# Stored rows scaled before they are stored, added in part by the vector engine and in part by accumulating transfers, and expert weights loaded in the order in which their buffers come free

## The reference

```python
g_top, g_idx = lax.top_k(softmax(t @ w_router_g + b_router_g), 1)        # one of 4 groups
e_top, e_idx = lax.top_k(e_logits of that group, 2)                      # two of its 8 experts
e_w = softmax(e_top) * g_top                                             # weight of each expert
for each expert e:
    hid = silu(t @ w1[e]) * (t @ w3[e]) * combine[:, e]                  # F = 256
    out = out + hid @ w2[e]
x = x + g2 * out
```

## Time and profile before

| | |
|---|---|
| time, median of 3 runs (lowest to highest) | 665.71 us (665.36 to 668.84) |
| the profiled execution's own time | 666.92 us |
| its span in the profile | 665.1 us |
| PE, DVE, ACT, POOL busy | 91%, 46%, 25%, 14% of the span |
| HBM read, written | 165.36 MB, 15.74 MB |
| weights loaded through SP's queue | 1 MB each, 23 to 24 us from issue to landing (median) |

### The profile page before, as it was taken

One profiled execution on the slowest core, in us unless ns is written; L12 is line 12 of the kernel. 1 busy time (PEld: TensorE's weight loads), 2 busy tenths in 40 slices (PEclk: granted clock), 3 DMA queues, 4 the chain that ended last, 5 costly groups with the idle time before them and its releaser, 6 DMA issues.

```text
span 665.1 us, 7868 instructions
## 1 busy us (share of the span) xinstructions
PE 604.8 (91%) x3008; PEld 361.3 (54%) x3008; DVE 304.1 (46%) x606; ACT 168.9 (25%) x368; POOL 93.7 (14%) x136
## 2 busy tenths in 40 slices
PE   2699797889999999999999989999999987989785
PEld 0444585667767677774588834454444433434233
DVE  0229989375454444119525384332232322245167
ACT  3024031034444425343202301232222211112010
POOL 2022241037600000000000020211111111100000
PEclk9999899879999999999999999999999998999899
DMA  8994945923180303051456674799999999999963
GB/s 313 398 356 176 337 146 181 378 99 126 61 320 1 127 1 127 1 191 61 183 242 272 214 312 150 299 410 422 419 421 419 420 419 419 423 418 422 387 260 127
DMA packets 41498, 173.85 MB, mean 261 GB/s; under 512 B 6268, under 2 KB 6332, under 8 KB 28660
## 3 DMA queue, kind: packets, MB, share of 16 engines
q1 hardware_dynamic: 34128, 159.40, 60.6%
q0 software_dynamic: 5744, 12.84, 5.4%
q10 hardware_dynamic: 1588, 1.10, 0.5%
HBM read 165.36 MB, written 15.74 MB: 272 GB/s over the span
## 4 chain that ended last, share of the span: by engine, by line
PE 62%; DMA 14%; DVE 8%; SPq 6%; issue 6%; POOL 3%; ACTq 1%; ACT 1%; DVEq 0%; POOLq 0%
PE bank L917 11%; PE bank L642 6%; PE bank L644 6%; PE bank L643 6%; PE bank L949 5%; DMA late<-in_w_dram 4%; DMA arena<-in_w_dram 4%; PE bank L732 4%; SPq L520 3%; POOL ss L1877 3%; DMA qkg<-in_k_norm_dram 2%; PE bank L822 2%; DMA late<-in_w_in_dram 2%; PE bank L932 2%; PE bank L823 2%
## 5 line engine op out<-in xcount | busy, mean ns | idle before, releaser
L917 PE MATMUL bank<-arena,hT 128*64 128x512 f32 x352 | 86.2, 631 | 8.5 <-DMA arena<-in_w_dram 7.5
L642 PE MATMUL bank<-hT_high,w_in_parts 128*128 128x512 f32 x160 | 67.0, 419 | 3.3 <-DVE w_in_parts L1330 3.3
L644 PE MATMUL bank<-hT_high,w_in_parts 128*128 128x512 f32 x160 | 63.7, 398 | 0.0
L643 PE MATMUL bank<-hT_low,w_in_parts 128*128 128x512 f32 x160 | 63.6, 398 | 0.0
L917 PEld LDWEIGHTS bank<-arena,hT 128*64 128x64 f32 x352 | 24.5, 142 | 50.0 <-issue 40.9
L1199 ACT COPY probs<-bank 128x512 f32<-128x512 f32 x32 | 18.7, 586 | 121.3 <-PE bank L917 121.3
L1606 DVE TENSOR_SCALAR hT<-bank,ab 128x128 f32<-128x128 f32 x64 | 21.8, 403 | 50.1 <-PE bank L902 50.1
L917 PE MATMUL bank<-late,hT 128*64 128x512 f32 x160 | 39.0, 632 | 3.6 <-DMA late<-in_w_dram 3.6
L949 PE MATMUL bank<-arena,g1b 128*64 128x512 f32 x176 | 39.7, 593 | 2.2 <-DVE g1b L1621 2.2
L932 PEld LDWEIGHTS bank<-fold,probs 128*128 128x128 f32 x256 | 32.7, 197 | 16.0 <-issue 11.4
L1364 DVE TENSOR_REDUCE st<-bank 128x2 f32<-128x256 f32 (+3 forms) x16 | 13.2, 824 | 57.9 <-PE bank L668 57.8
(11 more groups left out here) (285 smaller groups left out, 1007.0 us busy)
## 6 DMA issues: line engine op xcount, KB each, us to landing
arena<-in_w_dram SPq DMA_DIRECT2D x66, 1024.0 KB, 23.0
late<-in_w_dram SPq DMA_DIRECT2D x30, 1024.0 KB, 24.2
late<-in_w_ada_dram SPq DMA_DIRECT2D x6, 2048.0 KB, 12.7
arena<-in_w_ada_dram SPq DMA_DIRECT2D x5, 2048.0 KB, 9.6
arena<-in_w_in_dram SPq DMA_DIRECT2D x4, 2048.0 KB, 16.8
late<-in_w_in_dram SPq DMA_DIRECT2D x4, 2048.0 KB, 11.2
y_scratch<-route POOLq DMA_DIRECT2D x1, 4096.0 KB, 14.9
late<-in_w_out_dram SPq DMA_DIRECT2D x2, 2048.0 KB, 7.6
```

Source lines behind the costliest of these rows:

```text
L642: mm(bank[:, b, :], wH[:, b, k, :], hH[:, k, :], start=k == 0, stop=False)
L643: mm(bank[:, b, :], wH[:, b, k, :], hL[:, k, :], start=False, stop=False)
L644: last = mm(bank[:, b, :], wL[:, b, k, :], hH[:, k, :], start=False, stop=k == 7)
L917: last = mm(bank[r, 2 + n % 2, :].rearrange("p (w f) -> p w f", w=2), xgT[n // 2 % 2][:, k, SLOTS * (n % 2):SLOTS * (n % 2 + 1)], w13[s][: ...
```

## The change

It has three parts, all in the expert stage.

1. **Scaled rows.** The combine weights of all 16 pairs are found for each slot (`combine_weights`, `weight_sums`, `weights_by_slot`), and `drain_y` multiplies with them, so that what is stored in HBM is already scaled. The weights are made ahead of the one-hot tables of group 1 instead of behind two of them, and are 128x128 wide instead of 128x16. PE has 14 more groups of four small products.
2. **Adding the rows.** SP loads only tiles 0 and 1 of the stored rows, and does so once the last w2 has landed. DVE adds them with plain additions, half of them ahead of `drain_last(1)` and half behind the last `y_low`; nothing of it stands ahead of DVE's step 31 any more. Tiles 2 and 3 are added by four accumulating transfers of 0.5 MB that POOL issues straight from HBM into `xs`: two for j = 0 once SP's loads have landed, and two for j = 1 once those have landed. The one-hot matrices `spreadT` move from `near_end` to DVE's step 29. PE gets `keep_warm` products around its last two `gate_up`.
3. **Ring loads.** `load_pair(e)` issues w1 and w3 of experts e+1 and e+2 instead of e and e+1, ahead of w2 of e and e+1.

```diff
+BY_DVE = 2
             def load_pair(e):
-                for j in range(2):
-                    sp.wait_ge(ab_done, e + j + 1 - RING)
-                    load13(e + j, (e + j) % RING)
+                for n in range(e + 1, min(e + 3, E)):
+                    sp.wait_ge(ab_done, n + 1 - RING)
+                    load13(n, n % RING)
                 sp.wait_ge(y_done, e // 2 + 1 - RING // 2)
-                for j in range(2):
-                    load2(e + j, (e + j) % RING)
+                for n in range(e, e + 2):
+                    load2(n, n % RING)
             load2(5, 5)
-            sp.wait_ge(ab_done, 2)
-            load13(RING + 1, 1)
-            sp.wait_ge(y_done, 1)
-            load2(RING, 0)
-            load2(RING + 1, 1)
-            for e in range(RING + 2, E, 2):
+            for e in range(RING, E, 2):
                 load_pair(e)
...
-            rows_of(y_d, yg_loaded)
+            sp.wait_ge(w2_loaded[(E - 1) % RING], 16 * ((E - 1) // RING + 1))
+            for t in range(BY_DVE):
+                sp.dma_start(yg[:, t], y_d[2 * P * t:2 * P * (t + 1), :].rearrange("(p j) d -> p j d", j=2)
+                             ).then_inc(yg_loaded, 16)
...
+                    if g == 1:
+                        last = weight_sums(g, q)
+            def weight_sums(g, q):
+                e = 2 * (q - IDX_GROUPS[g][0])
+                for t in range(TT):
+                    lhs = place[g][t][:, e:e + 2, :].rearrange("p e s -> p (e s)")
+                    last = mm(bank[:, 7, W0 + 6 * q:W0 + 6 * q + 6], lhs,
+                              cparts[:, t, 2 * q:2 * q + 2, :].rearrange("p e c -> p (e c)"),
+                              start=t == 0, stop=t == TT - 1)
+                return last
             keep_warm(2, 5)
             slot_sums(0)
-            keep_warm(7, 5)
+            keep_warm(5, 5)
+            pe.wait_ge(weights_ready, 1)
+            for q in IDX_GROUPS[0]:
+                weight_sums(0, q)
+            keep_warm(2, 5)
...
             one_hot(0, range(TT))
             indices(0)
+            combine_weights()
             one_hot(1, range(0, 2))
...
-                    last = v.tensor_tensor(ysb[q % 3][:, w], bank[:, 6 + h, :], g2b[:, w], ALU.mult)
+                    last = v.scalar_tensor_tensor(out=ysb[q % 3][:, w], in0=bank[:, 6 + h, :], scalar=cws[:, q:q + 1],
+                                                  in1=g2b[:, w], op0=ALU.mult, op1=ALU.mult)
...
             all_experts(step, overflow_counts, near_end)
-            for t in range(2, TT):
-                dve.wait_ge(yg_loaded[t], 16)
-                add_stored(t)
+            def add_row(t, j):
+                v.tensor_tensor(xs[:, t, :], yg[:, t, j, :], xs[:, t, :], ALU.add).then_inc(x_added, 1)
+                dve.wait_ge(x_added, BY_DVE * j + t + 1)
+            dve.wait_ge(yg_loaded, 16 * BY_DVE)
+            add_row(0, 0)
+            add_row(1, 0)
             drain_last(1)
             for h in range(2):
                 y_low(1, h)
+            add_row(0, 1)
+            add_row(1, 1)
             for n in range(2 * TT):
                 t, w = n % TT, slice(CH * (n // TT), CH * (n // TT + 1))
                 dve.wait_ge(spread_done, n + 1)
+                if t >= BY_DVE:
+                    dve.wait_ge(rows_added, 32 * (TT - BY_DVE))
                 v.tensor_tensor(xs[:, t, w], bank[:, n, :], xs[:, t, w], ALU.add).then_inc(out_ready, 1)
...
+            pool.wait_ge(yg_loaded, 16 * BY_DVE)
+            for j in range(2):
+                if j == 1:
+                    pool.wait_ge(rows_added, 16 * (TT - BY_DVE))
+                for t in range(BY_DVE, TT):
+                    pool.dma_start(xs[:, t, :], y_d[2 * P * t:2 * P * (t + 1), :].rearrange(
+                        "(p j) d -> p j d", j=2)[:, j, :], accum_op=ALU.add).then_inc(rows_added, 16)
```

More of the change, by code:

```diff
@@ L374, in hybrid_trunk @@
         y_stored = [sem(f"y_stored{i}") for i in range(3)]
-        yg_loaded = [sem(f"yg_loaded{i}") for i in range(TT)]
         y_zeroed = sem("y_zeroed")
+        weights_ready = sem("weights_ready")
+        yg_loaded = sem("yg_loaded")
+        rows_added = sem("rows_added")
         zeros_ready = sem("zeros_ready")
@@ L567, in overflow @@
                 sp.sem_inc(x_turns, 1)
[L569 to L572, removed]
             def overflow_zeros():
@@ L955, in step @@
                     fold_halves(n - 1)
+                if n >= E - 2:
+                    keep_warm(2, 0, 0, CH // 2)
                 gate_up(n)
@@ L958, in step @@
                     down(n - 2)
+                if n == E - 1:
+                    keep_warm(2, 0, 0, CH // 2)
                 if n in ROWS_AT:
@@ L1574, in indices, with combine_weights @@
                 last.then_inc(sidx_ready, 1)
[L1576 to L1580, removed]
+            def combine_weights():
+                dve.wait_ge(exp_out, 1)
+                link(v.tensor_reduce(gsum, gexp, AX.X, ALU.add))
+                link(v.reciprocal(gsum, gsum))
+                dve.wait_ge(exp_out, 2)
+                link(v.tensor_scalar(best1, edif, 1.0, None, ALU.add))
+                link(v.reciprocal(best1, best1))
+                link(v.tensor_tensor(cw[:, 0, :], best1, gsum, ALU.mult))
+                link(v.tensor_tensor(cw[:, 1, :], cw[:, 0, :], edif, ALU.mult))
+                v.tensor_tensor(cwe, oh1, bc(cw[:, 0, :], S32, 2), ALU.mult)
+                link(v.tensor_tensor(cwr, oh2, bc(cw[:, 1, :], S32, 2), ALU.mult))
                 link(v.tensor_tensor(cwe, cwe, cwr, ALU.add))
                 for c in range(3):
[L1583 removed]
+                    last = v.tensor_copy(cparts[:, :, :, c], cwe)
                     if c < 2:
+                        link(last)
                         link(v.tensor_tensor(cwe, cwe, cparts[:, :, :, c], ALU.subtract))
+                last.then_inc(weights_ready, 1)
             def weights_by_slot():
[L1588 to L1592 removed]
+                parts = bank[:, 7, W0:W0 + 6 * PAIRS].rearrange("p (q c) -> p q c", q=PAIRS)
+                for x in range(2):
+                    r = slice(SLOTS * x, SLOTS * (x + 1))
+                    v.tensor_reduce(cws[r, :], parts[r, :, 3 * x:3 * x + 3], AX.X, ALU.add)
                 v.tensor_copy(toks, tokg[:, STORED:PAIRS])
@@ L1641, in drain_last @@
                     w = slice(CH * h, CH * (h + 1))
-                    last = v.scalar_tensor_tensor(out=ysb[q % 3][:, w], in0=bank[:, 6 + h, :], scalar=cws[:, i:i + 1],
+                    last = v.scalar_tensor_tensor(out=ysb[q % 3][:, w], in0=bank[:, 6 + h, :], scalar=cws[:, q:q + 1],
                                                   in1=g2b[:, w], op0=ALU.mult, op1=ALU.mult)
@@ L1669, in near_end @@
                     y_low(0, h)
-                dve.wait_ge(tok_iota, 1)
-                for i in range(LAST):
-                    last = v.tensor_scalar(spreadT[:, i].rearrange("p t q -> p (t q)"), iota_t, toks[:, i:i + 1], None,
-                                           ALU.is_equal)
-                last.then_inc(spreadT_ready, 1)
-                dve.wait_ge(yg_loaded[0], 16)
-                add_stored(0)
-                dve.wait_ge(yg_loaded[1], 16)
-                add_stored(1)
-            def step(n):
+            def step(n):
+                if n == E - 3:
+                    dve.wait_ge(tok_iota, 1)
+                    for i in range(LAST):
+                        last = v.tensor_scalar(spreadT[:, i].rearrange("p t q -> p (t q)"), iota_t, toks[:, i:i + 1],
+                                               None, ALU.is_equal)
+                    last.then_inc(spreadT_ready, 1)
                 if n == E - 2:
```

38 lines of the change are left out of this document (10 added, 28 removed).

## The result

The changed kernel takes 674.28 us (median of 4 runs, 669.59 to 675.16); the kernel before, run beside it, 665.75 (665.36 to 668.84). The ratio, taken over all the runs and not from these two medians, is 1.0103, with a 95% interval from 1.0056 to 1.015. Three of the four runs lie between 673.9 and 675.2 and one at 669.6. The forecast was 665.0, with a range from 660.3 to 672.0: the change is slower where no change was forecast, and the time lies outside the range. The profiled execution took 673.91 us, its span was 672.1.

What follows compares the result with a forecast made beforehand. Bound by DVE's last additions, behind them the full DMA engines. Last w2 at 635.6, SP's rows 642.0, POOL's rounds until 656.7, then 7.6 and 0.1: span 664.4, forecast 665.0 us, range 660.3 to 672.0.

Steps and rivals of the forecast that it cites:

- W': Landing of the last w2 in the changed kernel: 635.6, which is 2.0 earlier than 637.6 in the kernel before.
- Stored rows by POOL: Tiles 2 and 3 at the end: two rounds of accumulating transfers, 7.2 us each, done at 656.7.
- doubled price: POOL's round if each byte costs twice because the destination is read too: 8.1 us.
- Stored rows on DVE: SP's two loads after the last w2 land at 642.0; DVE's additions and drains then run until 651.2.
- The routing sums: Small products in gate_up(1) cost PE 1.2 us, DVE's weights 1.0 more; a lower clock adds 0, bounds 0 to 1.7.
- The ring loads: Expert 8's loads go 2.2 us earlier, filling the DMA gap at 424 to 428; the stream ends 2.0 earlier.
- the ring order gives nothing: Rival: small products at the lower clock delay gate_up(2) by 3 us, last w2 stays at 637.6; 667.0 us, chance 0.09.
- PE's end: gate_up(31) starts near 631, down(30) at about 638, ending by 642 to 644; 6 to 8 us less lateness.
- The one on the slower side: Rival: POOL's accumulating transfers cost more than double; decides at a round of 9.1, 10.5 gives 671.6 us; chance 0.20.
- The plain price: Rival: POOL's accumulating transfers cost no more than plain ones, rounds of 5.6 us, 661.8 us in all; chance 0.22.

Runs made afterwards that it cites:

- e2: The changed kernel with the old order of the ring loads: 675.44 us, ratio 1.0144 to the kernel before.
- e3: The changed kernel without the sums of the combine weights for pairs 0 to 13, those rows left unscaled: 668.76 us, ratio 1.0048 to the kernel before.
- e7: The changed kernel without SP's wait for the last w2 before loading stored rows: 669.15 us, ratio 1.0046 to the kernel before.
- e4: The changed kernel with POOL's four transfers overwriting instead of adding: 666.24 us, ratio 1.0009 to the kernel before.
- e9: The changed kernel without SP's wait for the last w2, and with POOL's transfers issued once all pairs are stored: 665.39 us, ratio 1.0004 to the kernel before.
- e1: The kernel before with the new order of the ring loads alone: 661.12 us, ratio 0.994.
- e10: The kernel before with the new ring order and its eight scaled additions moved behind expert 31's hidden values; no sums, hold or POOL transfers: 660.14 us, ratio 0.9904.
- e8: The changed kernel with all four tiles loaded by SP without the hold and added by DVE, no POOL transfers: 668.17 us, ratio 1.0025 to the kernel before.
- e5: The changed kernel with POOL's transfers issued once all pairs are stored, SP's hold kept: 672.01 us, ratio 1.0085 to the kernel before.
- e6: The changed kernel with all four tiles loaded by SP, still held, and added by DVE, no POOL transfers: 671.96 us, ratio 1.0086 to the kernel before.
- e11: The kernel before with twelve more groups of four small products in gate_up(1), results unused: 668.06 us, ratio 1.002.

## Why the prediction was wrong

The chain's end reads as forecast, DVE's wait between the pieces is there, and nothing else stands on the path behind the last w2. What failed are three terms of the sum: POOL's round, put at 7.2 us, the landing of SP's rows, put at 6.4 us behind the last w2, and the cost of a lower clock behind the new sums, put at 0. Against the predicted span of 664.4 the profiled one is 7.7 longer:

| term | predicted | measured | own share |
|---|---|---|---|
| last w2 lands (W') | 635.6 | 638.38 | +2.8 |
| SP's rows land, after W' | 6.4 | 8.6 | +2.2 |
| POOL's two rounds with waits | 14.7 | 18.5 | +3.8 |
| from there to the end | 7.7 | 6.6 | −1.1 |

- **Stored rows by POOL.** "I take a value nearer the doubled one, 7.2" is the largest miss. Measured are 9.15 and 8.76, above the doubled price of 8.1; in e2, e3 and e7 the same rounds take 8.8 to 9.4. e4 splits it: plain transfers take 6.07 and 6.61, not the 5.6 made from a single transfer's fixed part, and the add costs 2.6 more per MB. Bytes twice is right in size; the fixed part of two transfers in a round was some 0.7 too small, and there was no reason to choose below the full account of bytes. That account would have given 666.8 us (the prediction says 666.9), still 7.5 too little. The Trainium skill's page "Collectives: The Full Stack", section on the bandwidth ceiling, says that the add needs two source reads, which halves the rate of a reduction. The trace agrees in size (engines busy for 5.9 against 3.1 us by the same bytes), though it does not show the second read itself, and the price of 8.1 by that rule was nearer than mine.
- **Stored rows on DVE.** "Two MB take 4.9", with 1.4 fixed, gave 6.4; 8.5 us from the first issue to the last landing were measured, and 7.3 to 7.5 in e2, e3 and e4, which hold the rows alike. The fixed part of a small transfer did not carry over to two of one MB; the other microsecond is this execution's. DVE's own part was right: its first four additions and the drain ended well ahead of POOL's rows.
- **The routing sums.** The 1.2 us of products are there (from the first L923 group of `gate_up(1)` to the transposes 9.4 us, before 8.1), and DVE's weights take 3.6 us instead of 2.75, 0.9 more where 1.0 was forecast. But "bounds: 0 to 1.7 us for the rest of the stretch [...], I take 0" for the clock failed: `gate_up(2)` alone lost 1.9, above the upper bound, and the last w2 landed 3 to 5 us later in the executions with the lower clock than in those without. This is the term behind the late W'. Besides, the router's results were 1.6 later already ahead of any changed instruction (384.20 against 382.61), which is the execution and not the change: in e4 to e9, the same code up to there, they come between 381.97 and 383.33.
- **The ring loads.** Right as a step: e1 gains 0.6% and its gap closes. The last w3, forecast at 630.7, landed at 633.5, as late as W' (two MB stand behind it, not three). In the changed kernel's profiled execution the late `gate_up(2)` ate it, which is the mechanism of the rival "the ring order gives nothing"; in e4's, with the same code there, W' was 633.8, nearly 2 earlier than forecast.
- **PE's end.** `down(30)` ended at 645.4, forecast 642 to 644; it follows W', and PE is not on the path.
- **The rivals.** The one on the slower side named the right mechanism, the price of the round twice in an uncovered chain. It was to decide at a round of 9.1. The rounds were 8.96 on average, so the sign came from them together with the two terms ahead of them: two rivals came true at once. The plain price fell with e4's comparison. What the prediction did not price by itself is the hold: it took the landing after W' as given, where e7 shows that the wait costs some 4 us.

Without the wait, and with POOL early, the change comes level (e9); with the additions left to DVE in scaled form and only moved, and the ring order kept, it becomes 1.0% faster (e10). So the good part of the change is the ring order with the order of DVE's work. The accumulating transfers and the hold gave it back, but not they alone: e8 has neither and still lies 1.2% above e10. Between these two stand the sums with the lower clock, which e3 puts at about half of that, and DVE's one wait for all four tiles (until 648.0, in e10 for the first tile until 636.4). No run takes that wait, the `keep_warm` products or the earlier `spreadT` by itself.

## What to carry to other kernels

Think twice before making work wait for the last load of a stream: here the mean DMA share was 0.33 and 0.13 while its last pieces landed, and each round behind it was paid in full. Moving additions from an engine into the transfers costs their bytes a second time plus a fixed part a round, so compare that with the engine's time, and in a DMA-bound stretch expect it back in the loads (e5: the last w2 5.6 us slower). A closed gap in one window proves nothing until the mean over the whole stretch has been looked at. When an engine's work and the loads both bound the end, try the two edits together before judging each: here one alone was worth 0.6%, the other nothing, and both 1.0%, the last step barely clear of noise. And where one profile of a version lies far from another of the same code, look at the granted clock and at several executions before giving the difference to the edit.

## What the runs showed of the hardware

- An accumulating transfer from HBM into SBUF took 2.6 us more per MB than a plain one of the same shape (rounds of 9.15 and 8.76 against 6.07 and 6.61), with the same 288 packets and 1.05 MB in the profile and the engines busy for 5.9 against 3.1 us in the first round.
- The end of a stream tails off: with one w2 load and the rest behind it under way and nothing new issued, the DMA share fell from 0.89 (624 to 628) to 0.68, 0.33 and 0.13 (636 to 638) before the last landing.
- Around and behind the groups of small products PE's granted clock was at its lower level for ten microseconds and more in some executions (changed kernel 416 to 426, e6 413 to 427) and not at all in others of the same code there (e4, e7, e9: 1.00 from 400 to 440). The run times of e11 fell into two groups 4 us apart, of mean granted clock 0.954 to 0.968 and 0.971 to 0.976.
